# Three fp32r passes in place of an f32 matmul, for six of eight k-tiles of the experts' gate and up projections

## What is computed

```python
def moe(x, router_w, router_bias, w_gate, w_up, w_down):
    ...                                  # sigmoid scores, best group of 4, best 2 experts in it
    y = jnp.zeros_like(xt)
    for e in range(N_EXPERTS):           # 16 experts; w_gate, w_up 1024 x 512, w_down 512 x 1024
        h = jax.nn.silu(xt @ w_gate[e]) * (xt @ w_up[e])
        y = y + combine[:, e:e + 1] * (h @ w_down[e])
    return y.reshape(shp)
```

## Time and profile before

| what | us |
|---|---|
| time before, median of 3 (1578.92 to 1580.55) | 1580.51 |
| time of the profiled execution | 1581.12 |
| its span, first to last instruction | 1578.8 |
| PE busy, share of the span | 1350.4, 86% |
| PEld / DVE / ACT / POOL busy | 907.8 / 693.1 / 425.1 / 208.6 |
| experts of the first layer (504.18 to 844.70) | 340.52 |
| experts of the second layer (1184.99 to 1523.90) | 338.91 |

### The profile page before, as it was taken

One profiled execution on the slowest core, in us unless ns is written; L12 is line 12 of the kernel. 1 busy time (PEld: TensorE's weight loads), 2 busy tenths in 40 slices (PEclk: granted clock), 3 DMA queues, 4 the chain that ended last, 5 costly groups with the idle time before them and its releaser, 6 DMA issues. The chain is left out here.

```text
span 1578.8 us, 15547 instructions
## 1 busy us (share of the span) xinstructions
PE 1350.4 (86%) x5941; PEld 907.8 (57%) x5941; DVE 693.1 (44%) x1192; ACT 425.1 (27%) x667; POOL 208.6 (13%) x272
## 2 busy tenths in 40 slices
PE   5999878888995999999993289978959999999950
PEld 4989877854444555555551289843454555555530
DVE  2765345524244234443332823656442334333328
ACT  2533222220010222223332332262111333332213
POOL 3102142202000000000002200153001000000013
PEclk9999889995995999999996589998969999999985
DMA  6120140010616499999974511103264999999933
GB/s 182 54 81 28 54 146 1 1 48 11 216 72 226 166 363 354 368 361 357 357 267 149 188 54 54 69 39 110 80 232 147 331 358 357 355 356 357 329 118 118
DMA packets 132695, 296.52 MB, mean 188 GB/s; under 512 B 6608, under 2 KB 32937, under 8 KB 132640
## 3 DMA queue, kind: packets, MB, share of 16 engines
q1 hardware_dynamic: 120736, 252.77, 45.4%
q0 software_dynamic: 7296, 26.22, 4.7%
q10 hardware_dynamic: 4608, 16.78, 2.6%
HBM read 268.86 MB, written 26.89 MB: 187 GB/s over the span
## 5 line engine op out<-in xcount | busy, mean ns | idle before, releaser
L1001 PE MATMUL bank<-work 128*128 128x512 f32 x512 | 229.3, 601 | 5.5 <-DVE work L1986 5.5
L2006 DVE TENSOR_TENSOR WDN_LOW<-work,WDN_HIGH 128x1024 fp32r<-128x1024 f32 x120 | 141.4, 1220 | 201.6 <-ACT WDN_HIGH L1155 201.6
L1008 PE MATMUL bank<-work 128*128 128x512 f32 x512 | 225.0, 592 | 0.0
L1155 ACT ACTIVATE work<-bank 128x512 f32<-128x512 f32 (+4 forms) x180 | 79.4, 477 | 495.1 <-PE bank L1026 361.0
L1001 PEld LDWEIGHTS bank<-work 128*128 128x128 f32 x512 | 98.3, 193 | 118.6 <-issue 109.7
L1008 PEld LDWEIGHTS bank<-work 128*128 128x128 f32 x512 | 94.9, 190 | 108.1 <-issue 108.1
L1155 ACT ACTIVATE WDN_HIGH<-work 128x1024 fp32r<-128x1024 f32 x120 | 116.8, 1044 | 18.4 <-ACT work L1155 18.4
L1026 PE MATMUL bank<-WDN_HIGH,HT_HIGH 128*128 128x512 f32 x240 | 96.9, 404 | 0.0
L1026 PE MATMUL bank<-WDN_HIGH,HT_LOW 128*128 128x512 f32 x240 | 93.7, 390 | 0.0
L1026 PE MATMUL bank<-WDN_LOW,HT_HIGH 128*128 128x512 f32 x240 | 93.3, 389 | 0.0
L2301 POOL COPY idx_cur<-idx_all 128x1 int32 (+1 forms) x32 | 5.9, 185 | 657.4 <-PE bank L993 465.6
(11 more groups left out here) (438 smaller groups left out, 2537.1 us busy)
## 6 DMA issues: line engine op xcount, KB each, us to landing
work<-in_moe_w_gate_dram SPq DMA_DIRECT2D x32, 2048.0 KB, 14.6
work<-in_moe_w_up_dram SPq DMA_DIRECT2D x32, 2048.0 KB, 19.5
work<-in_moe_w_down_dram SPq DMA_DIRECT2D x32, 2048.0 KB, 9.9
y_rows<-work ACTq DMA_DIRECT2D x32, 512.0 KB, 8.3
work<-in_ab_w_in_dram SPq DMA_DIRECT2D x10, 1024.0 KB, 5.3
work<-in_c_w_in_dram SPq DMA_DIRECT2D x8, 1024.0 KB, 8.5
x_rows<-X SPq DMA_DIRECT2D x8, 512.0 KB, 2.6
work<-in_c_w_out_dram SPq DMA_DIRECT2D x1, 4096.0 KB, 12.7
```

Source lines behind the costliest of these rows:

```text
L1001: last = mm(bank[u][:, :], XGT[:, k, :], WGT[u][:, k, :], start=(k == 0), stop=(k == KD - 1))
L1008: last = mm(bank[2 + u][:, :], XGT[:, k, :], WUP[u][:, k, :], start=(k == 0), stop=(k == KD - 1))
L1155: return nc.scalar.activation(out, in_, ACT.Copy, scale=scale)
L2006: last = V.tensor_tensor(WDN_LOW[u][:, f, :], WDN[u][:, f, :], WDN_HIGH[:, f, :].bitcast(F32), ALU.subtract)
```

## The change

For k-tiles 0 to 5 of gate and up (three units of two k-tiles each, `UNITS = 3`), the f32 matmul gives way to three fp32r passes, as down has them; k-tiles 6 and 7 stay f32 and are added into the same bank (`plain`). For this

- ACT rounds each unit (128x1024) into one of four slots `GU_HIGH` (`round_units`), as soon as the weight has landed and the unit four before it was used (`gu_used`); DVE subtracts it from the weight in place, into `WGT_LOW` or `WUP_LOW` (`split_units`), and PE waits for each unit's `gu_split`;
- x comes out of the banks by ACT (`x_rounded`: `XGT_HIGH` in two copies, and the f32 tiles 6 and 7 in one), and DVE subtracts it from the banks (`x_split`, 128x512 and 128x256); h likewise (`h_rounded`, `h_split`), which drops one of ACT's copies of h;
- down is given back f-tile by f-tile (`down_used`, with f as the outer loop and the two halves inside), and the last expert's down runs in fp32r passes too;
- some semaphores of the second mixer are shared with the first.

SP's order of loads is the same. The core of the diff:

```diff
             def gate(l, pairs, u, g):
-                pe.wait_ge(xgt_ready, g * 2 + 2)
+                pe.wait_ge(xgt_ready, g + 1)
+                at_least(pe, sg_done, g - 1)
+                for n in range(UNITS):
+                    unit(bank[u][:, :], 2 * UNITS * g + n, (2 * UNITS * u + n) % 4, n, WGT_LOW[u])
                 pe.wait_ge(gate_in[u], arrivals(l, pairs))
-                at_least(pe, sg_done, g - 1)
-                for k in range(KD):
-                    last = mm(bank[u][:, :], XGT[:, k, :], WGT[u][:, k, :], start=(k == 0), stop=(k == KD - 1))
-                last.then_inc(gate_ps, 1)
+                plain(bank[u][:, :], WGT[u]).then_inc(gate_ps, 1)
...
+                def round_units(which, pairs, u, g):
+                    w, arrived, first = (WGT, gate_in, 0) if which == "gate" else (WUP, up_in, UNITS)
+                    act.wait_ge(arrived[u], arrivals(l, pairs))
+                    for n in range(UNITS):
+                        at_least(act, gu_used, 2 * UNITS * g + (first + n - 3))
+                        copy(GU_HIGH[(2 * UNITS * u + first + n) % 4][:, :, :], w[u][:, 2 * n:2 * n + 2, :]).then_inc(gu_rounded, 1)
...
-                def step(i, v):
+                def step(i, v, more=True):
                     u, g = (1 + v) % 2, i * 2 + (base + 1 + v)
+                    round_units("up", i + (v + 1), u, g)
+                    h_rounded(g - 1)
                     silu(u, g)
-                    h_copied(g - 1)
+                    if more:
+                        round_units("gate", i + 2, 1 - u, g + 1)
+                        x_rounded(g + 1)
+                    round_down(i + (v + 1), u, g)
                     result(i + 1, 1 - u, g - 1, i * 2 + v)
-                    round_down(i + (v + 1), u, g)
...
+                    split_units("up", u, g)
+                    h_split(g - 1)
+                    if more:
+                        split_units("gate", 1 - u, g + 1, range(UNITS - 1))
                     h_product(u, g)
-                    x_copied(g + 1)
+                    if more:
+                        split_units("gate", 1 - u, g + 1, range(UNITS - 1, UNITS))
+                        x_split(g + 1)
+                    split_down(u, g)
                     result(i + 1, 1 - u, g - 1)
-                    split_down(u, g)
```

More of the change, by code:

```diff
@@ L46 @@
 WORK = 35340
+UNITS = 3
 class Steps:
@@ L1018, in down @@
             def down(l, u, g):
[L1020 removed]
+                pe.wait_ge(ht_ready, g + 1)
                 at_least(pe, y1_out, g)
[L1022 to L1024 removed]
+                for f in range(4):
+                    pe.wait_ge(down_split, 4 * g + (f + 1))
+                    for half in (1, 0):
+                        cols = slice(512 * half, 512 * half + 512)
                         for n, (x, w) in enumerate(((HT_HIGH, WDN_HIGH), (HT_HIGH, WDN_LOW[u]), (HT_LOW, WDN_HIGH))):
@@ L1027, in down @@
                                       start=(f == n == 0), stop=(f == 3 and n == 2))
[L1028 to L1034, removed]
-                for half, done in ((1, y1_ps), (0, y0_ps)):
-                    for f in range(4):
-                        last = mm(bank[7 - half][:, :], HT[:, f, :], WDN[1][:, f, 512 * half:512 * half + 512],
-                                  start=(f == 0), stop=(f == 3))
-                    last.then_inc(done, 1)
+                    last.then_inc(down_used, 1)
             def experts(l):
@@ L1409, in experts @@
                     step(i, 1)
-                silu(1, base + 15)
-                h_copied(base + 14)
-                result(8, 0, base + 14, 14)
-                h_copied(base + 15)
+                step(NE // 2 - 1, 0, False)
+                h_rounded(base + 15)
                 result(8, 1, base + 15, 15)
@@ L1997, in result, with split_units @@
                     V.tensor_copy(YO[u][:, 512:1024], bank[6][:, :]).then_inc(y1_out, 1)
+                def split_units(which, u, g, some=range(UNITS)):
+                    w, low, first = (WGT, WGT_LOW, 0) if which == "gate" else (WUP, WUP_LOW, UNITS)
+                    for n in some:
+                        dve.wait_ge(gu_rounded, 2 * UNITS * g + (first + n + 1))
+                        high = GU_HIGH[(2 * UNITS * u + first + n) % 4][:, :, :].bitcast(F32)
+                        V.tensor_tensor(low[u][:, 2 * n:2 * n + 2, :], w[u][:, 2 * n:2 * n + 2, :], high, ALU.subtract)\
+                            .then_inc(gu_split, 1)
@@ L2019, in experts @@
+                split_units("gate", 1, base + 1, range(UNITS - 1))
                 h_product(0, base)
-                x_copied(base + 1)
+                split_units("gate", 1, base + 1, range(UNITS - 1, UNITS))
+                x_split(base + 1)
                 split_down(0, base)
@@ L2026, in experts @@
                     step(i, 1)
-                h_product(1, base + 15)
-                result(8, 0, base + 14)
+                step(NE // 2 - 1, 0, False)
+                h_split(base + 15)
                 result(8, 1, base + 15)
```

161 lines of the change are left out of this document (91 added, 70 removed).

## The result

The changed kernel takes 1609.74 us (median of 4 runs, 1607.76 to 1611.28) against 1580.53 (1578.92 to 1580.93) for the kernel before, run beside it: a ratio of 1.0185 [1.0169, 1.0201]. It is slower by 29.2 us. The forecast was 11.5 us slower; the direction and the mechanism hold, the size doesn't, and the time lies 2.7 us above the range. The profiled execution has a span of 1608.3 us (1578.8 before).

The account below looks back on a forecast made before the run. The chain from the gate weight's landing through ACT and DVE was taken to bound pairs of steps: seven pairs +7.6 us, start -2.2, end +0.3, so +5.7 a layer, +11.4 in both; 1592 us, range 1573 to 1607.

Parts of the forecast that it names:

- the landing at T + 15.2: Experts' steps: gate weight lands 15.2 us after T, the previous step's end; 0.7 us either way, 10 us of time.
- The deadline and the chain: Experts' steps: ACT waits for gate, DVE and PE wait behind it; two steps take 42.1 us against 41.0.
- ACT's wait: Middle of each step: ACT waits some 3 to 6 us for the DMA of the gate weight.
- The chain behind it: After gate lands: ACT's rounding, DVE's queue, PE's gate, up's rounding and split, PE to the end; 42.1 us a pair.
- the loop's hand-overs: Unit loops with counts in registers: 0 to 0.6 us in the chain, 4 us less or more in time.
- The clock: Stall before gate, up to 3.1 us, brings a 1.2 GHz stretch; gate loses 1.7 us, covered by 2.0 spare.
- Rival 2: Experts' steps: low clock not covered, 1.5 us more in each pair, 21 in all: 1613 us; chance 0.12.
- The start: Each layer to the end of step 1: four halves save 4.2 us, waits for x add 2.0; net -2.2.
- The end: Each layer's last down: fp32r saves 1.4 us, longer waits cost about 1.7; +0.3 us.
- PE's busy time: Experts: a sign of the prediction, PE's busy time falls by some 60 us in sum.
- The rule of about 358 GB/s: DMA in the steps: a core's HBM limit keeps each step at 20.5 us, 1577 us in all; chance 0.02.

Follow-up runs that it names:

- e1: Changed kernel with only SP's load order altered: next gate and up loads issued as soon as their buffers are free, ahead of down; 1529.74 us, ratio 0.9676.
- e3: Changed kernel with the three loads still issued together, but in the order gate, down, up; 1546.31 us, ratio 0.978.
- e11: Changed kernel with the three loads still issued together, but in the order down, up, gate; 1701.43 us, ratio 1.0778.
- e5: Changed kernel with 12 small matmuls ahead of PE's wait for x in the second step of each pair; 1613.37 us, ratio 1.0219.
- e4: Changed kernel with DVE waiting for the first gather's rows before splitting the first gate weight in each layer; 1606.19 us, ratio 1.0164.
- e10: Changed kernel with early gate and up loads, DVE waiting for the first gather, and the store after up's first rounding; 1524.15 us, ratio 0.9654.

## Why the prediction was right in its mechanism and wrong in its size

**What failed, in short.** The sum came out 18 us short, in three groups of terms: the landing at T + 15.2, which was T + 15.8 in the mean (8 us); start and end of each layer (4.5 us); and a hold-up of the first gather that was put at nothing (3.9 us). The first is the largest. The range reached up 15 us and was passed by 2.7, so with any one of the three right the time would have lain inside it.

**The deadline and the chain: right.** The text said that ACT would wait in the middle of each step for a weight issued at T, that DVE and PE would stand behind it, that steps would run in pairs, and that PE would idle before gate and before up. All of this is in the rows after; e1, e3 and e11 show that the landing decides. ACT's wait, put at 3 to 6 us, is 7.8 to 9.0 us in the short steps of the first layer and 1.6 to 2.7 in the long ones.

**The landing: the step that failed.** It stood in the sum as T + 15.2 and ACT's start at once. In the six pairs from 590 to 830 us ACT starts at T + 15.64, 15.77, 15.75, 16.06, 15.57 and 15.45; over all 14 pairs it is T + 15.45 to 16.58, 15.77 in the mean. That is 0.57 us late, with the weight of 14 some 8 us of time. In the pair shown it is T + 16.06, 0.86 late, of which 0.10 is the hand-over from DMA to ACT. The 14.4 us from issue to landing was right as a median of all loads (it is 14.4 after, too), but the load that decides is the first of a pair, and it took 15.2 us here and some 14.85 in the mean (an estimate, from ACT's starts less the issue and the 0.10). The prediction had allowed the landing 0.7 us either way, so this term by itself stayed within its bounds.

**The chain behind it: right.** From the end of ACT's first rounding to gate 5.20 us were forecast and 5.20 (735.87 to 741.07) measured; from gate to the rounding of up 6.0 and 5.99; to PE's up 2.2 and 2.37; from up to the step's end 12.15 and 12.30 (749.43 to 761.73). The pair shown takes 42.99 us for the 42.1 forecast, and 0.86 of the 0.89 is the landing. The mean pair is 299.2 / 7 = 42.7 us in the first layer and 297.8 / 7 = 42.5 in the second, in sum +5.3 and +3.9 us against the forecast. With the landing's 8 us taken off, about 1 us in 14 pairs is left for the loop's hand-overs, which were given 0 to 0.6 us each pair.

**The clock: right in the steps, missed around them.** One stretch at 0.50 per pair, ahead of it a stall of up to 4.3 us (3.1 forecast, since the landing is later), and no cost of its own there (e5). Rival 2, which had it uncovered, would have given 1613 us, a number close to the measured one; e5 shows that it isn't the reason, since at a clock of 1.00 the time stays. Whoever had only the time and the page's PEclk would have picked it. Outside the steps the clock did cost, as the next two points show.

**The start: too good by 0.4 and 2.1 us.** -2.2 us a layer were forecast. The stretch to the end of step 1 took 1.8 us less in the first layer (42.6 to 40.75) and 0.1 less in the second (41.8 to 41.7). The two layers differ by the clock. PE's wait for x ahead of the second expert's gate is 2.29 us in both, but in the second layer the matmuls behind it slow down (0.63 us a record, 0.43 apart):

```profile
1222.13 0.50 PE L1011 MATMUL bank<-GU_HIGH,XGT_HIGH 128*128 128x512 f32 x1 [2.29 <-DVE XGT_LOW_B L2019]
...
1224.35 0.63 PE L1011 MATMUL bank<-WGT_LOW,XGT_HIGH 128*128 128x512 f32 x1
```

Its 18 passes take 5.82 us (1222.13 to 1227.95) where they take 4.25 in the first layer (528.57 to 532.82). That is 1.6 us with nothing to cover it; the prediction had taken from the earlier trace rows that a short stall there leaves the clock up.

**The end: too good by 0.4 and 1.6 us.** +0.3 were forecast; the stretch from the end of step 15 to the last record grew by 0.7 (11.6 to 12.3) and 1.9 us (11.6 to 13.5). Timeline of the end of the first layer's experts, after:

```profile
848.23 0.63 PE L1039 MATMUL bank<-ident,work 128*128 128x128 f32 x4 [1.72 <-ACT work L1169]
...
851.32 0.79 PE L1051 MATMUL bank<-WDN_HIGH,HT_HIGH 128*128 128x512 f32 x1 [2.46 <-DVE HT_LOW L2030]
```

PE waits 1.72 + 2.46 = 4.18 us where it waited 0.78 + 1.18 = 1.96, so 2.2 us more where 1.7 were allowed. The last down itself was to save 1.4 us: it takes 7.3 us for 8.8 in the first layer, but 8.5 for 8.8 in the second, where its slow records last from 1545.06 to 1550.77.

**Not seen at all: POOL behind DVE.** The text looked for queues that stand behind a wait, but not for an engine that another slows down. The first gather costs 2.2 us in the first layer (e4), and the same hold-up stands at the start of the second, with +1.6 us between the layers.

**The sum once more**, measured less forecast: steps 5.3 + 3.9, start 0.4 + 2.1, end 0.4 + 1.6, gather 2.2 + 1.6, the kernel's end 0.6: 18.1 us. The span grew by 29.5 where 11.4 were forecast, 18.1 more.

**PE's work and DMA.** PE's busy time fell by 34 us, not by 60, because the stretches at the low clock count as busy; with the experts' steps at full clock (e10) it is 1283.5 us, 67 below the kernel before. The rule of about 358 GB/s, which had 0.02 of the chance, does not hold in these runs: e10's 398 GB/s over five slices on end would be impossible under it. The Trainium skill ("DMA: Bandwidth & Descriptors", Bandwidth) says that its higher rates, up to 425 GB/s, are those of a single core whose neighbour is idle. The runs, with one core at work and 398 GB/s, agree with that reading.

## What to carry to other kernels

When an engine takes over the preparing of an operand (a rounding, a split, a transposition), the deadline of its load moves ahead by that work and by all that stands in the same in-order queue; ask then where the load is issued, in which order, and what holds that issue back, and move it before the preparing is judged. The same change was worth -51 us (e1) or +29 us by the order of one queue. And where two causes each seem to cost nothing when taken away alone, take both away together: they may be covering each other.

## What the runs showed of the hardware

- GpSimd's small work is held up by DVE's subtraction of two 128x1024 tiles in SBUF: a copy of 128x1 takes 1.02 us for 0.19, the instruction of an indirect DMA 2.12 for 1.07. The Trainium skill ("SBUF — State Buffer", SBUF: two separate sides) says that a GpSimd operation that reads SBUF and a DVE operation with two SBUF inputs exclude each other for a whole instruction. The copy, which reads SBUF, agrees: it ends at 499.98 us, about where the first of the three subtractions that began at 498.72 does (3.49 / 3 = 1.16). For the indirect DMA no row shows which part of the instruction was held up.
- The weights' stream holds 398 to 399 GB/s over some 190 us (five slices) on one core (e10), with PE busy all of the time.
- A batch of three 2 MB loads lands in the order of its issues, the first after 8.8 to 10.7 us, the second after 13.5 to 14.4, the third after 19 to 21, whichever weight is which (e11, after, and e3 for the first and the third). Issued apart (e1), up lands after 10.4 and down after 10.2 us.
